# A two-layer transformer block on one core: the last token half's projections reordered, l2 norms by column sums, and expert sums taken one step later

## What is computed

```
def peer_ffn(xn, w_q, sub_keys, expert_u, expert_v):
    ...                              # 128 experts for each token, with gates g
    def chunk(args):                 # 128 tokens at a time
        xc, ec, gc = args
        u = expert_u[ec]
        act = jax.nn.gelu(jnp.einsum('cd,ced->ce', xc, u).astype(jnp.float32))
        return jnp.einsum('ce,ced->cd', gc * act, expert_v[ec])

def l2norm(x):
    return x * lax.rsqrt(jnp.sum(x * x, axis=-1, keepdims=True) + EPS)

def hybrid_layer(x, pre_norm_w, w_in, conv_w, a_log, dt_bias, gdn_norm_w,
                 w_branch_a, w_branch_b, w_out, post_norm_w):
    h = rmsnorm_2(x, pre_norm_w)
    proj = jnp.einsum('bsd,de->bse', h, w_in)
    (q_a, k_a, v_a, z_a, q_b, k_b, v_b, z_b,
     beta_logit, decay_logit, gate_a, gate_b) = jnp.split(proj, IN_OFFSETS, axis=-1)
    o_a = moba_attention(partial_rope(heads(q_a), pos), partial_rope(heads(k_a), pos), heads(v_a))
    y_a = jnp.einsum('bse,ed->bsd', o_a * jax.nn.silu(z_a), w_branch_a)
    qkv = jax.nn.silu(causal_dwconv(jnp.concatenate([q_b, k_b, v_b], axis=-1), conv_w))
    ...                              # g and beta from the logits
    o_b = gated_deltanet(...)        # l2norm(q), l2norm(k), a triangular inverse for each chunk
    y_b = jnp.einsum('bse,ed->bsd', rmsnorm_2(o_b, gdn_norm_w) * jax.nn.silu(z_b), w_branch_b)
    merged = jax.nn.sigmoid(gate_a) * y_a + jax.nn.sigmoid(gate_b) * y_b
    return x + rmsnorm_2(jnp.einsum('bsd,de->bse', merged, w_out), post_norm_w)
```

## Time and profile before

| what | us |
|---|---|
| median of 3 runs (1382.16 to 1389.08) | 1382.6 |
| the profiled execution | 1377.14 |
| its span in the trace | 1375.3 |
| loop, pairs 0 to 63: 218 to 584 | 366 |
| loop, pairs 64 to 127, to the end of the last sum: 584 to 1059.1 | 475.1 |
| the end: 1059.1 to 1375.3 | 316.2 |

### The profile page before, as it was taken

One profiled execution on the slowest core, in us unless ns is written; L12 is line 12 of the kernel. 1 busy time (PEld: TensorE's weight loads), 2 busy tenths in 40 slices (PEclk: granted clock), 3 DMA queues, 4 the chain that ended last, 5 costly groups with the idle time before them and its releaser, 6 DMA issues.

```text
span 1375.3 us, 14070 instructions
## 1 busy us (share of the span) xinstructions
PE 1099.7 (80%) x5130; PEld 545.3 (40%) x5130; DVE 816.1 (59%) x1849; ACT 450.3 (33%) x1246; POOL 288.9 (21%) x261
## 2 busy tenths in 40 slices
PE   6989995877786666678877799875888798798687
PEld 2877672432252222123333343323333354454353
DVE  5475656887946998463456765566553317535531
ACT  1121223555433344352334433433342213113111
POOL 0000002434343535433222232331321000000000
PEclk9987977999998999999999899998989899899798
DMA  9995507999999999999999799997988475156132
GB/s 392 328 388 198 199 0 274 336 353 395 383 384 422 420 405 391 422 421 422 420 422 403 270 420 421 421 421 287 421 331 346 180 276 214 66 212 259 76 123 76
DMA packets 63664, 433.14 MB, mean 315 GB/s; under 512 B 6979, under 2 KB 10348, under 8 KB 11884
## 3 DMA queue, kind: packets, MB, share of 16 engines
q0 software_dynamic: 36864, 268.45, 48.4%
q1 hardware_dynamic: 26064, 161.76, 30.0%
q10 hardware_dynamic: 668, 2.04, 0.4%
HBM read 431.17 MB, written 1.06 MB: 314 GB/s over the span
## 4 chain that ended last, share of the span: by engine, by line
PE 44%; DVE 25%; DMA 21%; ACT 7%; issue 3%; POOL 1%; ACTq 0%; SPq 0%; DVEq 0%; POOLq 0%
DMA AR<-in_puv,idx 18%; PE ps L1055 17%; PE ps L1010 8%; DVE AR L1619 8%; PE ps L704 4%; PE ps L1161 2%; PE ps L926 2%; DMA W<-in_w_mod 2%; PE ps L1036 1%; DVE rowb L1766 1%; PE ps L954 1%; DVE tok L1802 1%; DVE rowb L1802 1%; DMA X<-in_x 1%; ACT av L2128 1%
## 5 line engine op out<-in xcount | busy, mean ns | idle before, releaser
L2377 POOL DMA_INDIRECT AR<-in_puv,idx x256 | 288.5, 1127 | 752.7 <-PE ps L1010 501.5
L1010 PE MATMUL ps<-AR,acc 128*64 128x512 f32 x912 | 288.3, 668 | 124.8 <-ACT acc L2011 123.9
L1619 DVE CUSTOM_DVE_ANT_0 AR<-AR,mixT 128x1024 f32<-128x1024 f32 x128 | 153.3, 1222 | 84.2 <-DMA AR<-in_puv,idx 83.9
L1055 PE MATMUL ps<-W,AR 128*128 128x512 f32 x416 | 197.2, 614 | 3.2 <-ACT AR L2011 2.2
L1010 PEld LDWEIGHTS ps<-AR,acc 128*64 128x64 f32 x912 | 72.2, 146 | 293.3 <-ACT acc L2011 201.5
L1619 DVE CUSTOM_DVE_ANT_0 AR<-AR,tok 128x1024 f32<-128x1024 f32 x128 | 153.2, 1220 | 58.6 <-DMA AR<-in_puv,idx 58.5
L2126 ACT ACTIVATE av<-av 128x1 f32<-128x1 f32 x256 | 51.6, 201 | 353.1 <-DVE av L1619 352.8
L1055 PE MATMUL ps<-W,hT 128*128 128x512 f32 x320 | 155.1, 616 | 6.0 <-ACT rowb L2011 6.0
L1055 PEld LDWEIGHTS ps<-W,AR 128*128 128x128 f32 x416 | 77.6, 197 | 81.5 <-issue 76.0
L1055 PEld LDWEIGHTS ps<-W,hT 128*128 128x128 f32 x320 | 57.5, 194 | 85.5 <-issue 76.8
L704 PE MATMUL ps<-hT,W 128*128 128x256 f32 x320 | 76.8, 403 | 8.7 <-DVE AR L1343 6.1
(11 more groups left out here) (434 smaller groups left out, 1331.0 us busy)
## 6 DMA issues: line engine op xcount, KB each, us to landing
W<-in_w_in SPq DMA_DIRECT2D x90, 1024.0 KB, 9.0
W<-in_w_mod SPq DMA_DIRECT2D x24, 1024.0 KB, 11.1
W<-in_wba SPq DMA_DIRECT2D x8, 1024.0 KB, 8.2
W<-in_wbb SPq DMA_DIRECT2D x8, 1024.0 KB, 8.1
W<-in_wo SPq DMA_DIRECT2D x8, 1024.0 KB, 8.0
W<-in_w_out SPq DMA_DIRECT2D x4, 1024.0 KB, 5.9
W<-in_wq SPq DMA_DIRECT2D x4, 1024.0 KB, 7.0
AR<-in_puv,idx POOLq DMA_INDIRECT x256, 11.1
```

The source lines that it names most:

```text
L1010: t = mm(of(("E", a, c))[64 * g:64 * g + 64, :], dg_at((2 * p + g) % NDG, late), GB[:, places[g], D + c * 512:D + c * 512 + 512], start=(m ...
L1055: t = mm(b[:, :], src[:, k, :], slab(i)[:, k, :], start=(k == 0), stop=(k == 7))
L1619: ttr(GB[:, n, 0:D], GB[:, n, 0:D], H2[a][g], 1.0, 0.0, MUL, ADD, av[:, a, c:c + 1]).then_inc(*ve.sig("dot", p, g))
L2377: eng.indirect_dma_start(GB[:, n, :], None, puv, bass.IndirectOffsetOnAxis(ap=idx[:, a, c:c + 1], axis=0)).then_inc(*gp.dma(f"g{n}", "gat" ...
```

## The change

- `ORDER` is one list for each half. In half 0 the convolution's inputs come as v_b, q_b, k_b. In half 1 all six of them come first, then q and k, v, z_b, z_a, and last `ga`, `ba`, `gb`, `bb` and `o` without small steps between, except turns. The inverse of each group so stands between other projections.
- Half 0's chores stop, within the loop, at `ob_turn` of group 1. What is left (the second halves of both `bb`, both `o`, `finish`: 19 chores, 12 pieces) is `held`: two of it are done before the last `accumulate`, the others are mixed with the norm of half 1.
- `conv_turn` on DVE keeps only the small copy; the taps are the chores `conv_lo` (three operations) and `conv_hi` (four), with a buffer of their own.
- The l2 norm: `l2_mm` is four matmuls with a moving operand of one column; `l2_root` takes root and reciprocal of 128x4 and 128x8 and makes two diagonal matrices; `l2_spread` multiplies them by ones (two matmuls of 128x512) and DVE multiplies from PSUM.
- From the pair on at which the ring has seven places, `accumulate` comes one step later in half 0 too (before: in half 1 only), and waits for the weights of both groups.
- Costs of chores now come from two tables; a pair's share is 1/64.
- `z_b` and `gb` of half 1 get buffers that are not shared; waits follow the new order.

```
-    if a == 0:
-        do("accumulate", p, places, bool(state["late"]))
-    else:
-        if lag:
-            do("accumulate", *lag)
-        lag = p, places, True
+    if lag:
+        do("accumulate", *lag)
+    lag = p, places, bool(state["late"])
+    if not state["seven"]:
+        do("accumulate", *lag)
+        lag = None
...
     def accumulate(p, places, late):
-        if a:
+        if late:
             pe.wait_ge(("dg", p, 0), ("dg", p, 1))
...
+    assert not rest
+    last = second_last()
+    for _ in range(2):
+        do(*held.pop(0))
     do("accumulate", *lag)
-    last = second_chores(1)
-    while rest or last:
+    while held:
+        for _ in range(1):
+            do(*last.pop(0))
         for _ in range(2):
-            if rest:
-                do(*rest.pop(0)[1])
-        if last and (not rest or last[0][1][0][:2] == "x2"):
-            do(*last.pop(0)[1])
+            if held:
+                do(*held.pop(0))
+    for chore in last:
+        do(*chore)
...
-    proj("za", 0, [("mt", 2) if two else ("mpv", 1)], [("conv_turn", 2, 0)], [("l2_mm", 1, 0), ("conv_silu", 2, 0), ("l2_scale", 0)],
...
+    proj("za", 0, [("conv_turn", 1, 0), ("conv_silu", 0, 0)], [("conv_lo", 1, 0), ("l2_mm", 0, 0), ("conv_hi", 1, 0)], [("conv_silu", 1, 0)])
```

The l2 norm on PE:

```
             def l2_mm(a, j, n):
...
-                mm(b[:, :], ones, sq[a], start=True, stop=True).then_inc(*pe.sig("l2_mm", a, j, n))
-
-            def l2_scale(a, n):
+                for q in range(4):
+                    t = mm(b[:, q:q + 1], sq[a][:, q * P:q * P + P], ones[:, 0:1], start=True, stop=True)
+                t.then_inc(*pe.sig("l2_mm", a, j, n))
+
+            def l2_root(a, n):
...
+            def l2_spread(a, n):
+                for j in range(2):
+                    b, old = take(("l2s", a, j, n), (("l2_q", "l2_k")[j], a, n))
+                    pe.wait_ge(*old, ("l2_dg", a, j, n))
+                    mm(b[:, :], ones, dgl[a][:, j, :], start=True, stop=True).then_inc(*pe.sig("l2_sp", a, j, n))
```

On DVE, the taps (`conv_lo` is the part before) and the l2 norm:

```
+            def conv_hi(a, j, n):
+                dst, tmp = conv_to(a, j, n), heads(tapped[a])
+                ve.wait_ge(("conv_lo", a, j, n))
+                t = link(tap(a, j, n, 2, tmp))
+                ve.wait_ge(t)
+                t = link(tt(dst, dst, tmp, ADD))
+                ve.wait_ge(t)
+                t = link(tap(a, j, n, 3, tmp))
+                ve.wait_ge(t)
+                tt(dst, dst, tmp, ADD).then_inc(*ve.sig("conv2", a, j, n))
...
+            def l2_root(a, n):
+                ve.wait_ge(("l2_root", a, 0, n), ("l2_root", a, 1, n))
+                t = link(rec(lr[a], lr[a]))
...
+                ve.wait_ge(t)
                 for j in range(2):
...
+                    tt(heads(dgl[a][:, j, :]), ident.unsqueeze(1).to_broadcast([P, 4, P]),
+                       lr[a][:, 4 * j:4 * j + 4].unsqueeze(2).to_broadcast([P, 4, P]), MUL).then_inc(*ve.sig("l2_dg", a, j, n))
+
+            def l2_spread(a, n):
+                for j in range(2):
+                    o = qk[a, n][:, :, 1 - j, :]
+                    ve.wait_ge(("l2_sp", a, j, n))
+                    stt(o, o, (0.5 * DK, 0.5)[j], heads(of("l2s", a, j, n)[:, :]), MUL, MUL).then_inc(*ve.sig(("l2_q", "l2_k")[j], a, n))
```

And its roots on ACT:

```
-            def l2_scale(a, n):
+            def l2_root(a, n):
                 for j in range(2):
-                    ac.wait_ge(("l2_mm", a, j, n), *([("l2_k", a, 0), ("l2_q", a, 0)] if n else [("x2_gain", 0, 1)]))
-                    act(rt[a][:, j, :], of("l2", a, j, n)[:, :], ACT.Sqrt, scale=0.25, bias=eps).then_inc(*ac.sig("l2_root", a, j, n))
+                    ac.wait_ge(("l2_mm", a, j, n), *([("l2_dg", a, 1, 0)] if n else []))
+                    act(lr[a][:, 4 * j:4 * j + 4], of("l2", a, j, n)[:, 0:4], ACT.Sqrt, scale=0.25, bias=eps
+                        ).then_inc(*ac.sig("l2_root", a, j, n))
```

More of the change, by code:

```diff
@@ L183, with cost, __init__, do @@
 UNITS = [(a, g, r) for a in range(2) for g in range(2) for r in range(2)]
-PIECE, HOP, SPREAD = 1.75, 0.9, 65.0
-def second_chores(a):
-    out = []
-    def do(name, *what, cost=HOP):
-        out.append((cost, (name, a, *what)))
-    def proj(key, n, *between, k0=0, k1=8):
+PE_TIME = {"proj": 1.75, "beta": 1.4, "products": 2.6, "inv_t": 1.8, "norm_h": 1.8}
+VE_TIME = {"x2_norm": 1.3, "x2_out": 1.3, "norm_h": 1.2, "decay": 3.5, "ms": 1.5, "conv_lo": 2.1, "conv_hi": 2.8, "conv_silu": 1.4,
+           "l2_root": 1.6, "l2_spread": 1.4, "za_out": 1.4, "bb_out": 1.4, "dec": 2.1, "products": 2.9, "inv_start": 2.1, "inv_t": 1.7,
+           "gain_out": 1.5}
+def cost(chore):
+    return max(PE_TIME.get(chore[0], 0.9), VE_TIME.get(chore[0], 0.7))
+class Chores:
+    def __init__(self, a):
+        self.a, self.out = a, []
+    def do(self, name, *what):
+        self.out.append((name, self.a, *what))
+    def proj(self, key, n, *between, k0=0, k1=8):
         for q, k in enumerate(range(k0, k1, 2)):
-            do("proj", key, n, k, k + 2, cost=PIECE)
+            self.do("proj", key, n, k, k + 2)
             if k == 6:
-                do(*taken(key, n), cost=0)
+                self.do(*self.taken(key, n))
             for chore in between[q] if q < len(between) else ():
-                do(*chore, cost=0 if chore[0] in ("conv_silu", "l2_scale") else HOP)
-    def taken(key, n):
+                self.do(*chore)
+    def taken(self, key, n):
         if key in ("q", "k"):
@@ L253, in second_chores @@
-    proj("bb", 0, hops[12:13], hops[13:14], k1=4)
-    proj("bb", 1, hops[14:15], hops[15:16] + two * [("rest", 1)], k1=4)
-    for name in ("new_values", "read_out") if two else ("new_values", "state", "read_out"):
-        do(name, 1)
-    do("gain_out", 1)
-    do("ob_turn", 1)
+    proj("ba", 1, hops[14:15], hops[15:16], [("new_values", 0)], [("state", 0)])
+    proj((2, 1), 1, [("read_out", 0)])
+    proj((0, 1), 1, [("conv_turn", 2, 1)], [("conv_lo", 2, 1)], [("conv_hi", 2, 1)])
+    proj((1, 1), 1, [("conv_turn", 0, 1), ("conv_silu", 2, 1)], [("conv_lo", 0, 1)], [("conv_hi", 0, 1)])
@@ L259, in second_chores @@
+    for hop in hops[14:16] + [("new_values", 1), ("state", 1), ("read_out", 1), ("gain_out", 1), ("ob_turn", 1)]:
+        do(*hop)
+    n = len(c.out)
     proj("bb", 0, k0=4)
@@ L267, in loop_chores @@
 def loop_chores():
     out = []
-    idx, gw, state = set(), set(), {"keys": 0, "late": False, "six": None, "open": False}
+    idx, gw, state = set(), set(), {"keys": 0, "late": False, "six": None, "seven": False, "open": False}
     ring = [(n, ("first", n)) for n in range(5)]
@@ L405, in loop_chores @@
     h1, h2, second, spread = half1(pair), 0, False, 0
-    rest = second_chores(0)
-    share, spent, lag = sum(cost for cost, _ in rest) / SPREAD, 0.0, None
+    rest, held = second_first()
+    share, spent, lag = sum(map(cost, rest)) / 64, 0.0, None
     for p in range(P):
@@ L438, in loop_chores @@
         if state["six"] and not state["open"]:
-            state["six"] = None
+            state["six"], state["seven"] = None, True
             ring.append((6, ("sixth", *state["last"])))
```

202 lines of the change are left out of this document (117 added, 85 removed).

## The result

The changed kernel takes 1345.6 us (median of 4 runs, 1342.39 to 1348.19) against 1385.4 us of the kernel before beside it on the same chip: a ratio of 0.971 (95% interval 0.967 to 0.975), 40 us less. A second comparison on another chip gave 0.973 (0.970 to 0.976). The forecast was 1332, in a range of 1313 to 1358, with 50.8 us less; four fifths of that came. The profiled execution of after took 1345.45 us, its span is 1343.7, which is 31.6 less than that of before. The 40 of the medians and the 31.6 of the spans differ because the profiled execution of before (1377.14) lay 8 us under the median of the runs, and that of after on its median.

What follows compares the result with a forecast made beforehand. The loop was taken as bound by DMA bytes, with holes, and the end by PE. Terms 1039.3 + 22.6 + 255.8 + 6.8 gave 1324.5 against 1375.3, -50.8 us; from the 1382.6 median that is 1332, range 1313 to 1358.

Steps and rivals of the forecast that it cites:

- The end: Stretch from half 1's first projection on, bounded by PE: 255.8 us instead of 292.2, -36.4, with 9 us of waits.
- DVE as the bound of the convolution stretch: Rival in the end's first stretch: DVE's 7.4 us per projection grow to 9, PE waits 25 us; 1348, chance 0.15.
- Pairs 64 to 127: Second half of the gather loop: fewer holes (-18 us) and fewer bytes (-12.4 us) bring the last landing to 1024.5.
- Bytes: Pairs 64 to 127: held projections release no slots in the loop, 2.5 slabs of 2.1 MB fewer, -12.4 us.
- Holes: Pairs 64 to 127: the two DMA holes at l2_scale shrink, 8 of 26 us remain: -18 us, bounds 0 and -23.
- The rival that the holes stay: Pairs 64 to 127: table changes and three-engine chains make the holes, which only move; +18, 1350, chance 0.17.
- the one of a better case: Rival: holes of 3 us, waits of 3 us, the last sum 4 us sooner; -15, 1317, chance 0.13.
- Half 0's sums one step later: Pairs 19 to 63: sums delayed one step while the DMA queue is full; taken as 0 us, bounds -5 and +10.
- the slower rival: Pairs 19 to 63: routing on DVE lengthens steps, the queue empties once per pair; 58 us lost, 1390, chance 0.03.
- the rival of a later sum that harms a little: Half 0: the later sum does not help, since DMA is full there anyway; +10, 1342, chance 0.06.
- The last sum: From the last landing to the last sum's end, behind read-out, turn and two pieces: 14.8 us instead of 4.2, +10.6.
- From the last sum to half 1: From the last sum to half 1's first projection: held pieces hide the norm, 22.6 us instead of 17.2, +5.4.

Runs made afterwards that it cites:

- section 4: Changed kernel with the costs of half 0's norm root and scaling set to 3.0, so `norm_h` stands in pair 66, not 65: 1339.0 us, ratio 0.969.

## Why the prediction was right or wrong

**The end: right.** 255.2 us against 255.8. PE's clock was 1.00 throughout, its work 243.95 us with the four us for the l2 norm (forecast 246.8), and 11.3 us idle (forecast 9). DVE as the bound of the convolution stretch did not come; a wait of 2.5 us is the longest. No run takes the new order of the end back by itself: that it is worth these 37 us rests on the rows before and after. The four one-column matmuls of a column sum took 0.95 and 1.05 us at two places, against 1.0 in the forecast. That 1.0 came from a small misreading: the twelve of the earlier trace rows take 2.7 us and not 2.9, which is 0.9 for four.

**Pairs 64 to 127: right in the sum and in both parts.** 438.5 us against 440.5. Bytes: 392 GB/s over the 470.9 us before is 184.6 MB, 411 over 438.5 after is 180.2 MB, 4.4 MB or 10.4 us less at 421 GB/s (forecast 12.4). Holes: the remaining 22 of the 32.4 us (forecast 18, bounds 0 and 23). That the reciprocals were a part of it is shown by the run that puts them back, 8 to 11 us; the other 11 to 14 of the 22 have no run of their own. The rival that the holes stay is out; so is the one of a better case, though its mechanism is not, as the run with the norm spread shows: one hole of the new order cost 3 to 6 us, and was no term of the sum. Moving the costs of chores packs others together, and I looked only at the place that the change was about.

**Half 0's sums one step later: wrong, though inside its bounds (-5 and +10).** I argued that the DMA queue has slack for one step and that nothing else is touched. The step that failed is "PE only meets each sum after the small steps of the next pair": a small step can wait, here 3.3 and 4.4 us for DVE, and everything behind it on PE waits too. Routing steps on DVE stood in the prediction under the slower rival, as a reason for a longer step, in nearly all pairs; they act at two places (485 to 495 and 545 to 555), and the delay costs 3.5 to 5.3 us in all. That is the rival of a later sum that harms a little (chance 0.06, +10) at half its size, by another mechanism than it names. Taking the delay over from pairs 64 on was the wrong witness: there is no routing there, and that the delay does no harm there was never tested. The sum behind `norm_h` (section 4) and the gather that waited 19.09 us in the kernel before stood behind a wait of PE in just this way. The Trainium skill ("TensorE: Matmul & The Clock Gate", Architectural detail: the array is 16× 32×32, not 1× 128×128) says that PE may pull weight loads ahead of matmuls in flight. The rows show that this was no help here: the matmuls of the sum kept their place behind the spread and began at 540.21. The 8.5 us of the profile divide so: 1.4 lie ahead of pair 0, 3.7 in pairs 0 to 15 (unexplained), 1.0 from 16 to 18, and of the stretch that the term is about, -0.8 from pair 19 to 45 and 3.2 from 45 to 63.

**The last sum: wrong by 11.0 us.** Two steps of the term failed. The first: I counted 3.3 us from the landing until the squares of the read-out can begin, for the last dots and weights alone. In the program's order PE still has a level of the inverse, the new values, a sum of 3.41 us, the state and the read-out to do, and DVE has steps of the first two ahead of the last dots, each waiting for PE; 7 us passed before the first dot, and 11.5 before the read-out ended. That is 8.2 of the 11.0. I had read DVE's row ahead of the squares and not ahead of the dots. The second: two pieces at 3.4 us took 6.10, another 2.7. PE had idled 4.50 us for the turn and worked in short pieces before, and the clock was at 0.74 in that stretch. The squares to the turn (4.5), and the sum itself (1.9), came as forecast.

**From the last sum to half 1: 24.9 against 22.6**, with a wait of 3.00 us for a copy ahead of the `o` pieces where 1.1 was taken. The norm was hidden, as forecast.

**The forecast for the median.** I put it against 1382.6; the kernel before had medians of 1383.4 to 1386.6 beside the later runs, and its profiled execution lay 6 to 9 us under them. The 31.6 us of the spans are 40 in the medians, and with that the missing 19 are 11. Those 8 us are luck: they come from which execution of the kernel before was profiled, and no step of the forecast earned them.

## What to carry to other kernels

A step that is moved past another on an in-order engine takes over that step's waits. Before moving one later "because there is slack", list what then stands ahead of it, and look up each one's longest wait, not its duration. When a stream ends (the last gathers), the chain to place is not that from the last transfer but what is queued ahead of it on every engine: finish independent chains a few steps sooner. And if a planner's costs are changed, look through its whole output for steps that now stand together, not only the ones that the change is about.
